# One key tile for all new tokens, and rotary scores of the cached keys in four column strips

## The reference, cut to what matters

```
lat = concat(cache_lat[pages] (4096 x 128), lat_new (1 x 128))
kr  = concat(cache_kr[pages]  (4096 x 32),  kr_new  (1 x 32))
kv  = lat @ w_ukv                       # 8 heads x (64 key + 64 value) columns
k_nope = rms_norm(kv[..., :64])         # per key and head
sc  = (q_nope . k_nope + q_rope . kr) * scale      # over 4097 keys, 8 heads
out = softmax(sc) @ v
```

## Time and profile before

| | us |
|---|---|
| median of 3 runs | 964.74 (963.88 to 965.33) |
| span of the profiled execution | 963.0 |
| attention units 0 to 7 | about 183 to 497 |
| one middle unit, pv to pv | 39.5 |

### The profile page before, as it was taken

The page is one execution under the profiler, slowest core; times in us unless marked ns, Lnnn a source line. Parts: engine busy times, 40 slices in busy tenths (PEclk is TensorE's granted clock), DMA queues, the critical chain, the costliest instruction groups (busy, mean ns, idle before and its releaser), DMA issues.

```text
span 963.0 us, 20520 instructions
## 1 busy us (share of the span) xinstructions
PE 932.5 (97%) x7954; PEld 872.2 (91%) x7954; DVE 648.3 (67%) x1241; ACT 527.2 (55%) x1188; POOL 190.4 (20%) x191
## 2 busy tenths in 40 slices
PE   5899999999999999999999999999999999999998
PEld 3588876799999999999899989999999999999997
DVE  2893378588798987988873667777777777713221
ACT  2414845798989889898872344444444443312111
POOL 0031223323433334333440210010000011000000
PEclk9999999999999999999999999999999999999999
DMA  9986633300221202202121433333333332652202
GB/s 336 325 271 221 219 132 106 138 2 24 88 92 42 88 24 97 102 24 89 45 67 45 110 59 89 88 87 87 95 99 100 97 87 60 171 134 61 65 3 90
DMA packets 106819, 100.16 MB, mean 104 GB/s; under 512 B 7135, under 2 KB 95471, under 8 KB 104654
## 3 DMA queue, kind: packets, MB, share of 16 engines
q1 hardware_dynamic: 102950, 77.91, 27.7%
q0 software_dynamic: 3456, 20.97, 6.1%
q10 hardware_dynamic: 340, 0.27, 0.1%
HBM read 96.41 MB, written 2.94 MB: 103 GB/s over the span
## 4 chain that ended last, share of the span: by engine, by line
PE 88%; DVE 4%; ACT 3%; DMA 2%; issue 1%; SPq 0%; POOL 0%; DVEq 0%; ACTq 0%; POOLq 0%
PE ps L917 51%; PE ps L1303 19%; PE ps L912 7%; DMA RW<-w_ada 2%; PE ps L950 2%; PE ps L1210 2%; PE ps L1261 2%; PE ps L1298 1%; PE ps L1089 1%; PE ps L923 1%; PE ps L1236 1%; DVE input_low L1940 1%; ACT qrot L1725 0%; DVE up_weights_low L2363 0%; DVE RB L2379 0%
## 5 line engine op out<-in xcount | busy, mean ns | idle before, releaser
L917 PE MATMUL ps<-normed_high,up_weights_high 128*128 128x260 f32 x704 | 142.5, 284 | 0.1
L917 PE MATMUL ps<-normed_high,up_weights_low 128*128 128x260 f32 x704 | 142.5, 284 | 0.0
L917 PE MATMUL ps<-normed_low,up_weights_high 128*128 128x260 f32 x704 | 142.2, 284 | 0.0
L855 POOL TENSOR_TENSOR latents_low<-RB,latents_high 128x512 fp32r<-128x512 f32 (+1 forms) x72 | 86.2, 1197 | 168.8 <-ACT latents_high L1682 160.3
L1303 PE MATMUL ps<-key_weights_high,latents_high 128*128 128x260 f32 x528 | 116.4, 302 | 0.8 <-ACT RB L1729 0.7
L1798 ACT ACTIVATE up_weights_high<-RW 128x1024 fp32r<-128x1024 f32 x44 | 46.5, 1060 | 128.0 <-PE ps L917 128.0
L917 PEld LDWEIGHTS ps<-normed_high,up_weights_high 128*128 128x128 f32 x704 | 108.9, 189 | 0.6 <-DVE normed_low L2384 0.6
L917 PEld LDWEIGHTS ps<-normed_high,up_weights_low 128*128 128x128 f32 x704 | 109.2, 190 | 0.0
L917 PEld LDWEIGHTS ps<-normed_low,up_weights_high 128*128 128x128 f32 x704 | 108.7, 189 | 0.0
L1303 PE MATMUL ps<-key_weights_high,latents_low 128*128 128x260 f32 x528 | 106.3, 283 | 0.0
L1303 PE MATMUL ps<-key_weights_low,latents_high 128*128 128x260 f32 x528 | 106.2, 282 | 0.0
(11 more groups left out here) (335 smaller groups left out, 2107.0 us busy)
## 6 DMA issues: line engine op xcount, KB each, us to landing
RW<-w_ada SPq DMA_DIRECT2D x24, 1024.0 KB, 7.5
RW<-w_up SPq DMA_DIRECT2D x44, 512.0 KB, 5.0
RW<-w_down SPq DMA_DIRECT2D x8, 1408.0 KB, 7.1
RW<-w_in SPq DMA_DIRECT2D x11, 512.0 KB, 6.6
RB<-w_o SPq DMA_DIRECT2D x8, 512.0 KB, 4.3
RB<-x_prompt SPq DMA_DIRECT2D x2, 1024.0 KB, 13.2
o_y_p<-RB SPq DMA_DIRECT2D x4, 448.0 KB
cst<-consts SPq DMA_DIRECT2D x1, 845.0 KB, 12.6
```

The costliest lines, as they stand in the source:

```text
L855: nc.gpsimd.tensor_tensor(latL[:, g % 3, c:4 * P], turned[:, g % 3, c:4 * P], latH[:, g % 3, c:4 * P].bitcast(F32), ALU.subtract).then_inc ...
L917: last = mm(ps[j % 4][rows[0]:rows[1], h, 0:H], lhsT, src[:, h * H:(h + 1) * H], start=start, stop=stop)
```

## The change

Three things are changed in the attention stage.

- **One tile for all new tokens.** The 33rd tile of each sample goes: `KTILES` = 32, `NG` = 8, and with it its DMA, GpSimd's copies and clears, and the mask. In unit 0 only, TensorE computes the scores of all 8 new tokens against all samples' queries (`new_token_scores`, behind (1, 0)) and their keys (`new_token_keys`, one f32 matmul of 512 columns, behind (4, 0)); ScalarE and VectorE make their rstd and a column of scores, of which a diagonal mask leaves each sample its own. `scores_max` copies that column (8 wide) in as a 33rd set of scores. pv keeps 33 matmuls; the last reads the 8 rows `new_lat`.
- **Rotary scores in strips.** L1298 goes, and so does the rotary keys' transpose in every group. Instead there are two new jobs "r" per unit (`ROPE_AT` = groups 2 and 4): four transposes each turn 16 tiles of rotary keys, and ScalarE copies 512 columns to `kr_turned`. One group later, ahead of the products of tile 1, four f32 matmuls with `QBD` as weights (32 columns) and 128 moving columns each write their scores to four 32-row strips (`rope_products`); ScalarE copies them (128 columns) to `rope_scores`; ahead of the products of tile 3 one transpose turns them back (`turn_rope_scores`), and ScalarE copies 128 columns to the score buffer `srd`.
- **`turn_head`** moves from the start of the unit to behind tile (0, 0).

The core of the diff, without the constants, buffers and the steps of the new tokens' column:

```diff
-KTILES = PAGES + 1
+KTILES = PAGES
+ALLT = KTILES + 1
-NG = 9
-GT = [4] * (NG - 1) + [1]
-UNIT = NG + KTILES
+NG = 8
+GT = [4] * NG
+ROPE_AT = (2, 4)
+UNIT = NG + KTILES + len(ROPE_AT)
...
         order.append(("t", g + 2) if g + 2 < NG else ("tn", g + 2 - NG))
+        if g in ROPE_AT:
+            order.append(("r", ROPE_AT.index(g)))
         order += [("k", 4 * g + n) for n in range(GT[g])]
...
+            def rope_products(u, r, j):
+
+                kfree(pe, key_job(u, "r", r))
+                for n in range(4):
+                    mm(kslot(j)[GROUP * n:GROUP * n + GROUP, 0, KWW:KWW + P], QBD[:, u, :, :].rearrange("p c h -> p (c h)"), kr_turned[:, n, :], start=True, stop=True)
+
+            def turn_rope_scores(u, r, j):
+
+                kfree(pe, key_job(u, "k", 4 * ROPE_AT[r] + 5))
+                tr(kslot(j)[:, 1, KWW:KWW + P], rope_scores, P)
...
                         kclaim(j)
-                        if n == 0:
-
-                            mm(kslot(j)[:, 0, KWW:KWW + 4 * HEADS], turned[:, g % 3, 4 * P:5 * P], QBD[:, u, :, :], start=True, stop=True)
-                        at = P * (4 - GT[g] + n)
+                        if n == 1 and g - 1 in ROPE_AT:
+                            rope_products(u, ROPE_AT.index(g - 1), j)
+                        if n == 3 and g - 1 in ROPE_AT:
+                            turn_rope_scores(u, ROPE_AT.index(g - 1), j)
...
+                        if (g, n) == (0, 0):
+                            turn_head(u)
+                        if (g, n) == (1, 0):
+                            turn_max(u) if u > 0 else new_token_scores()
...
+                        if (g, n) == (4, 0):
+                            pv(u) if u > 0 else new_token_keys()
...
+                    if g in ROPE_AT:
+                        j = key_job(u, "r", ROPE_AT.index(g))
+                        kfull(act, j)
+                        A(kr_turned[:, :, :].rearrange("p g n -> p (g n)"), kflat(j)[:, 0:4 * P], ACT.Copy).then_inc(key_free[j % 3], 1)
...
+                        if n == 1 and g - 1 in ROPE_AT:
+                            A(rope_scores, kslot(j)[:, 0, KWW:KWW + P], ACT.Copy)
+                        if n == 3 and g - 1 in ROPE_AT:
+                            r = ROPE_AT.index(g - 1)
+                            A(srd[u % 2][:, P * r:P * r + P], kslot(j)[:, 1, KWW:KWW + P], ACT.Copy)
```

More of the change, by code:

```diff
@@ L71 @@
 for _name, _n in (("ident", P), ("ones", P), ("blk", P), ("perm", QK), ("mask", P), ("spread", P), ("cos", T),
-                  ("sin", T), ("tail", 1), ("quarter", 1), ("pick", HEADS), ("cosq", 5 * ROPE // 2), ("sinq", 5 * ROPE // 2)):
+                  ("sin", T), ("quarter", 1), ("pick", HEADS), ("cosq", 5 * ROPE // 2), ("sinq", 5 * ROPE // 2)):
     CC[_name] = _c
@@ L103, in constants @@
     c[NOPE + half:QK, CC["sin"]:CC["sin"] + T] = np.sin(ang)
-    c[1:, CC["tail"]] = NEG
     c[:, CC["quarter"]] = q % 4
@@ L252, in bank_jobs @@
             for name in BANKS[b]:
-                if (name in OF_FORMER and u > 0) or (name not in OF_FORMER and u < NS):
+                if name in OF_FORMER and u > 0 or name in OF_FIRST and u == 0 or name not in OF_FORMER + OF_FIRST and u < NS:
                     at[b][name, u] = len(at[b])
@@ L376, in build @@
         wv = RB[:, 3636:3636 + HEADS * VD].rearrange("p (h d) -> p h d", h=HEADS)
-        turned = RB[:, 9040:9040 + 3 * 5 * P].rearrange("p (g n) -> p g n", g=3)
+        turned = RB[:, 9040:9040 + 3 * 4 * P].rearrange("p (g n) -> p g n", g=3)
+        rope_scores = RB[:, 9040 + 3 * 4 * P:9040 + 3 * 4 * P + P]
         kwH, kwL = parts_at("key_weights", [P, 2, 2, KWW], rb_at + 4 * 6256)
         snd_all = [RB[:, 8336 + 288 * e:8336 + 288 * e + 288] for e in range(2)]
-        assert 288 == KTILES * HEADS + GROUP - HEADS and 6256 + 8 * KWW == 8336 and 8336 + 2 * 288 <= 9040
-        snd = [x[:, 0:KTILES * HEADS] for x in snd_all]
-        srd = [ut_free[:, 0:264], RB[:, 12656:12920]]
-        ssd = [fs_free[:, 264 * e:264 * e + 264] for e in range(2)]
+        assert 288 == ALLT * HEADS + GROUP - HEADS and 6256 + 8 * KWW == 8336 and 8336 + 2 * 288 <= 9040
+        snd = [x[:, 0:ALLT * HEADS] for x in snd_all]
+        srd = [ut_free[:, 0:KTILES * HEADS], RB[:, 12656:12656 + KTILES * HEADS]]
+        ssd = [fs_free[:, 264 * e:264 * e + KTILES * HEADS] for e in range(2)]
         mx = [fs_free[:, 528 + 8 * e:536 + 8 * e] for e in range(2)]
@@ L422, in build @@
         n_lat = KTILES * P
-        n_kr = 36 * ROPE
+        n_kr = PAGES * ROPE
         lat = [RW[:, e * n_lat:(e + 1) * n_lat].rearrange("p (c d) -> p c d", c=KTILES) for e in (1, 0)]
-        kr_ = [RW[:, 2 * n_lat + e * n_kr:2 * n_lat + (e + 1) * n_kr].rearrange("p (c d) -> p c d", c=36) for e in range(2)]
+        kr_ = [RW[:, 2 * n_lat + e * n_kr:2 * n_lat + (e + 1) * n_kr].rearrange("p (c d) -> p c d", c=PAGES) for e in range(2)]
+        kr_turned = RW[:, 2 * (n_lat + n_kr):2 * (n_lat + n_kr) + 4 * P].rearrange("p (g n) -> p g n", g=4)
+        assert 2 * (n_lat + n_kr) + 4 * P <= 10752
         sb("hidden_tail", [P, max(8, (rb_at + 4 * 2 * FT * T - nc.sbuf_base) // 4)])
@@ L830, in _ @@
                 cached_latents(n, n)
-            for e in range(2):
-                nc.gpsimd.memset(lat[e][:, PAGES, :], 0.0).then_inc(s_clr, 1)
-                nc.gpsimd.memset(kr_[e][:, PAGES:36, :], 0.0).then_inc(s_clr, 1)
             for k in range(1, LT):
@@ L883, in _ @@
                         low_latents(u + 1, g + 2 - NG)
-                    if u == 0 and g == 1:
-                        pool.wait_ge(s_clr, 4)
-                        pool.wait_ge(s_new, 16)
-                        for n in range(2):
-                            new_key(n, n)
-                            new_latent(n, n)
                     if u == NS - 1 and 2 <= g < 2 + LT:
@@ L1258, in pv @@
                 mm(bank("pv")[:, KV:KV + HEADS], ones, pd[e], start=True, stop=True)
-                for n in range(KTILES):
+                for n in range(ALLT):
                     r = GROUP * (n % 4)
-                    last = mm(bank("pv")[r:r + GROUP, 0:KV], snd_all[e][:, HEADS * n:HEADS * n + GROUP], lat[e][:, n, :], start=(n < 4), stop=(n >= KTILES - 4))
+                    rows = P if n < KTILES else NS
+                    last = mm(bank("pv")[r:r + GROUP, 0:KV], snd_all[e][0:rows, HEADS * n:HEADS * n + GROUP], lat[e][:, n, :] if n < KTILES else new_lat,
+                              start=(n < 4), stop=(n >= ALLT - 4))
                 last.then_inc(is_full("pv"), 1)
@@ L2267, in turned_probs, with new_token_column @@
                     at += w
+            def new_token_column():
+                own = new_scores[0:NS, :, :]
+                nope, rope = [new_parts[:, a:a + NS * HEADS].rearrange("p (b h) -> p b h", b=NS) for a in (0, NS * HEADS)]
+                dve.wait_ge(s_new, 3)
+                st.seq(V.tensor_tensor(own, nope, new_rstd.unsqueeze(1).to_broadcast([NS, NS, HEADS]), MUL))
+                st.seq(V.tensor_tensor(own, own, rope, ADD))
+                st.seq(V.tensor_tensor(own, own, new_mask.unsqueeze(2).to_broadcast([NS, NS, HEADS]), ADD))
             def unit(u):
```

112 lines of the change are left out of this document (66 added, 46 removed).

## The result

The changed kernel takes 975.95 us (975.06 to 976.51), the kernel before on the same chip 964.31: a ratio of 1.0119, 95% interval 1.0104 to 1.0133. The forecast was 968.0 with a range of 960.5 to 973.0. The sign was right, the size was not.

A forecast was written before the change was run, and what follows sets the result against it. TensorE was taken as the bound; six middle units +2.2, unit 0 +1.1, unit 7 +0.8 and -0.8 behind the loop gave +3.3 on a 963.0 us span, so 968.0 with 1.7 between span and median; range 960.5 to 973.

The forecast's parts named there:

- work removed: TensorE, per unit: 33rd tile 0.72, nine L1298 1.98, two transposes 0.22 go; sum 2.92 us.
- strips, two bursts: TensorE, per unit: eight strip matmuls at pv's pace, 0.5, plus 0.05 a burst for filling and draining: 0.60 us.
- transposes back: TensorE, per unit: two transposes turning the strip scores back, 0.22 us.
- old wait at group 1: Start of group 1: TensorE's existing wait for k1, 0.57 us by starts, goes when `turn_head` stands behind k0.
- wait at `head_scores`: Behind k4: TensorE waits for ScalarE's two copies of the turned head; 0.35 us, an estimate between 0 and 0.57.
- wait A: At k16: TensorE waits for k15's slot, freed late by the chain behind p20; 1.52 us in each of eight units.
- wait B: Ahead of k15: the transpose back waits for ScalarE's square of k13 and its copies; 0.65 us a unit.
- wait C: Group 5: the transpose back waits for k21's slot, 1.13 us after its end, k22 covering 0.72; 0.41 and 0.10.
- Moving `turn_head` moves 0.87 us and changes no sum: `turn_head` goes behind tile (0, 0): the claim that TensorE's summed work stays the same.
- Once: Work outside the per-unit terms: unit 0's new-token matmuls 1.5 us, its old k17 wait (0.9) gone, unit 7 +0.4.
- ScalarE becomes the bound: Rival: ScalarE's backlog reaches k13 1 us later, wait B becomes 1.6 us, 975 us; chance 0.13 for 971 to 978.
- my three signs of being wrong: k16's idle under 1 us, a transpose back waiting over 1 us, or TensorE waiting for the latents' DMA.

The follow-up runs named there:

- r1_one_group_later: The changed kernel with the second job of rotary keys, r(1), in group 5 instead of group 4: 962.94 us, ratio 0.9997 to the kernel before.
- strips_undone: The changed kernel with rotary scores made as before (no jobs r, strips or transposes back), the new tokens' tile and `turn_head`'s place kept: 953.16 us, ratio 0.9882.
- both_moves: The changed kernel with r(1) in group 5 and the strip products ahead of tile 0 instead of tile 1: 956.49 us, ratio 0.9921.
- r_between_tiles: both_moves with the two jobs r moved from the group's start to between tiles 1 and 2 of groups 2 and 5: 959.23 us.

## Why the prediction was wrong

By its own terms, a middle unit:

| term | forecast | after |
|---|---|---|
| work removed | -2.92 | -2.92 |
| strips, two bursts | 0.60 | 1.09 |
| transposes back | 0.22 | 0.22 |
| old wait at group 1 | -0.57 | -0.57 |
| wait at `head_scores` | 0.35 | 0.24 |
| wait A | 1.52 | 1.76 |
| wait B | 0.65 | 0.26 |
| wait C | 0.51 | 0.55 |
| pv's last matmul, 8 rows | 0 | 0.13 |
| k8 | not seen | 0.26 |
| k26 | not seen | 0.37 |
| sum | +0.36 | +1.39 |

The mean unit measured +1.41, so the table closes. Some 1.05 us a unit were missing; times eight that is 8.4, against the 8.0 between forecast and median.

- **What bounds the kernel, and wait A: right.** The place, the chain and the releaser are as forecast, and r1_one_group_later shows it to be the slot order. Its size was 0.24 short, 0.16 of it ScalarE's copy to `srd` in k15. I had counted this copy as load and not as a link of the chain. Most of the rest is the step from the end of the freeing copy to TensorE, 0.15 (365.46 to 365.61) where I had 0.06.
- **C right; B too large.** In the trace before, ScalarE starts k13's square 0.27 ahead of k14's end (356.22 and 356.49), and I took TensorE and ScalarE to be delayed alike. After, it starts 0.78 ahead (360.73 and 361.27 + 0.24): TensorE is held up by the burst and the wait at k8, and ScalarE less; which of the two does more was not tried. The square and the copy of the strips (0.48 and 0.16) are as forecast, the last step to TensorE is 0.37 (361.37 to 361.74) and not 0.24.
- **The strips: the term that failed first.** "I take the pv row because form and strips are the same" holds for the pace (four more cost 0.22) and not for a burst of four. I added 0.05 for filling and draining, and it was 0.3. No row of the trace before held a lone burst of this form. The measured 1.09 lies inside my bounds of 0.5 to 1.76, but the forecast took the lower end, and its range had no room for the middle. By the Trainium skill, TensorE: Matmul & The Clock Gate, section Measured speedup vs the span model, I had an estimate of 0.37 a burst. Directly behind pv a burst adds 0.35, near to it, while four more in a running burst cost 0.22 and a lone burst 0.55; neither the estimate nor my 0.30 holds the ends of a burst.
- **"Moving `turn_head` moves 0.87 us and changes no sum": true of TensorE's own work only.** For the waits I had 0.22 net a unit. In the changed kernel its place is worth 1.1, since the 33rd tile that went was also a cover.
- **The step that was missing: the waits of 0.2 to 0.4.** I followed three waits with care and took all other slots to be as they were. New jobs turn the slots for every tile, and each of them has its own margin. They make 0.63 a unit. That they come with the form is shown by strips_undone.
- **Where these two come from.** The rows of the changed kernel place both. k8 stands in k7's slot, which is used again 1.06 after k7's end (352.54 to 353.60), and only 0.88 of transposes stand between; with the steps of wait C less its strip copy (0.25, 0.48, 0.18, 0.06) and the 0.10 of restart I could have forecast 0.19 there. k26 stands in the slot of the latents turned at the start of its group. ScalarE's last copy out of it ends 2.52 behind k23's end (334.66 to 337.18), about as in strips_undone (2.46), but TensorE has 0.33 less to do ahead of k26: the transpose and the 32-column matmul that the strips saved. There the saving came back as a wait. (In r1_one_group_later the burst stands in that group, ahead of k25, and k26 does not wait.) This is read from rows and not tried by a run, the wait at `head_scores` stays open, and two attempts to remove the short waits only moved them.
- **Once.** The new tokens' scores and keys took 0.6 and 1.2 us by starts, together 0.3 over the 1.5 forecast; the wait for the maximum behind the loop is gone, as forecast; TensorE never waited for the latents' DMA.
- **The rivals.** "ScalarE becomes the bound" gave 975, near the measured time, and by a mechanism that isn't there: B was 0.26 and not 1.6. That a time fits is no proof of a cause.

The chance for slower by over 0.2% was the largest, 0.53. The range failed since its upper end was built from one backlog and held no allowance for terms that I had not listed. And none of my three signs of being wrong showed (k16's idle was 1.5, no transpose back waited over 1 us, nothing waited for the DMA): they tested the waits that I had listed, and the loss lay in a price and in waits that I had not.

## What to carry to other kernels

A job of another kind that is put into a ring of three slots shifts which tile waits for which. List, for every tile of the period, the job three back and what stands between, with the copies that precede the freeing one, before counting the saved matmuls. Price a short burst of another matmul form by a lone burst (0.55 us for four here, 0.22 for four more) and not by the pace of a long one. And read an undone version as a candidate: here the change without its strips is 1.2% faster than the kernel before, while the whole is 1.2% slower.

## What was not expected of the hardware

The granted clock of TensorE falls to half for short stretches outside the attention stage, and in other places in each kernel. Busy time by stretch, granted clock in the third last column, of both_moves and of r_between_tiles:

```profile
500.00:505.00 5.00, 5.00 (x53) 4.84 (x54) 1.59 (x5) 0.80 (x2) 0.00 (x0) 1.00 0.34 101
555.00:560.00 5.00, 5.00 (x34) 4.87 (x34) 5.00 (x8) 2.45 (x4) 0.00 (x0) 0.66 0.13 31
```

```profile
500.00:505.00 5.00, 5.00 (x46) 4.75 (x45) 0.78 (x3) 0.33 (x1) 0.00 (x0) 0.73 0.29 82
505.00:510.00 5.00, 5.00 (x20) 4.48 (x20) 0.77 (x1) 1.89 (x4) 0.00 (x0) 0.58 0.35 105
```

In shorter stretches of r_between_tiles the clock is 1.00 up to 502 us and 0.50 from 502.5 to 509. A mean of 0.73 is full clock (2.4 GHz) in part and half clock (1.2 GHz) in part, so the time lost is the stretch's length times 1 less the mean. r_between_tiles loses 5 x 0.27 + 5 x 0.42 = 3.4 us right behind the last pv, where both_moves loses nothing; TensorE was busy all the time there. But both_moves loses 1.7 at 165 us, where r_between_tiles doesn't, so the net is 1.8. Summed in this way from 150 to 950 us, the profiled executions lose between 1.7 and 6.8 us (before and after 3.4 each, so that comparison is not touched; both kernels with a second copy 6.8, both_moves 3.4). The profiled execution of r_between_tiles is 2.8 us longer than that of both_moves: 1.8 by the clock, and 0.1 in each of eight units. Those with a second copy are 5.3 and 5.4 longer, 3.4 of it by the clock. The medians rest on other executions too, for which this was not summed; it is why I judge differences under 3 us between versions by the units. What decides where the clock falls was not tried.
